# Second mixer: merge gates projected between the products of the linear attention's levels, gates kept in a slot of the weight ring

## The chip, the cores and the metric

The kernel runs on one core of a Trainium2 chip, in fp32 throughout. The metric is the device time of one execution in microseconds, the median of some runs. Five engines work side by side and wait for each other through semaphores: TensorE (PE: matmuls and transposes into PSUM), VectorE (DVE), ScalarE (ACT: functions and copies), GpSimd (POOL) and SyncE (SP), which issues nearly all transfers of weights from HBM. PSUM has 8 banks of 512 fp32 columns.

## The reference, cut to what matters

Two stacks of blocks run one after the other on 256 tokens of width 1024. The second has one layer: a hybrid mixer, then a mixture of 32 experts. The change touches the mixer alone:

```python
proj = jnp.concatenate([hc, hx], axis=1) @ w_in          # q k v | zd | b a | hq | f (2 directions) | hi | hz | gates (2 x 1024)
odn  = deltanet scans of q, k, v, b, a                    # gated delta rule, both directions
ohg  = gla scans of hq, f, hi (tokens in column order)    # HGRN2, both directions
br_dn = gated_rmsnorm(odn, zd, dn_norm_g) @ w_br_dn
br_hg = gated_rmsnorm(ohg, hz, hg_norm_g) @ w_br_hg
y = (sigmoid(gate_dn) * br_dn + sigmoid(gate_hg) * br_hg) @ w_out
x = x + mod_x[2] * y                                      # then norm, router, 32 experts (2 per token)
```

`silu(z)` gates each normed output, the two `sigmoid` gates (1024 columns each) weigh the two branches before the output projection. The gates depend on the layer's input alone, not on the scans.

## The kernel before, in words

**Weights.** `ring` has six slots of 2 MB. Every weight block of the mixer is one load of 2048 KB by SyncE into slot number mod 6, in the order of `plan2`: k, v, q, zd, hq, f0, hi, f1, hz, gd0, gd1, gh0, gh1, brd, brh, wo0, wo1 (`COL` gives the columns of w_in). A load waits for the reader of what was in its slot before (`READ`, the pair behind each entry); SyncE takes the loads strictly in order. Slots 0 to 2 are also the working memory (`spare`) of half the deltanet chunks, so loads into them wait for `S_ready` 6. After the plan come the experts' blocks (`main_pairs`): six blocks for each pair of experts, with eight places (`block_of`): the six slots in the order `SEQ`, and two areas of the arena. The first eight go as the places come free, each later one when the block eight before it has been read.

**Order of TensorE.** It is written out by hand. After the deltanet's ticks (the last work in them is `state` of chunk 3): zd (4 chains of 8 matmuls of 256 columns, banks 0 and 1), the sum of squares `o_ss`, hq (banks 4, 5), then for each direction d: f (512 columns, banks 4 to 7); for d = 0 hi (banks 0 to 3), for d = 1 hz (banks 4, 5) and gd0 (6, 7); transposes of the decayed keys (`kdT_ready`, L1294) that ScalarE copies out as `kdTok`; the state sum (`Sg_sum`, bank 2); eight levels; `attX` (L1323, bank 3); the output sum `og` (banks 0, 1). A level l is 8 products of 128x128 (L1316) into banks 4, 5 or 6, 7. For it GpSimd makes differences of log decays (L2573), ScalarE their exponentials, VectorE multiplies queries and keys with them (L2011, L2012: `W_ready`) and takes the product over into `attT` under the level's mask (L1994: `att_masked`). After the second direction: `o_ss` (L1339), the gates gd1, gh0, gh1 (banks 2, 3 or 0, 1), which ScalarE passes through the sigmoid one by one into `sgt`, an area of the arena, then the branch products brd and brh (each 8 chains of 4 matmuls), the broadcast of a row (L1364), and wo0, wo1. The norm, the router and the pairs of experts (L832 up, L847 down) follow.

**Semaphores.** `SHARED` lists, engine by engine, the order of increments of shared semaphores. `at(name, n)` is the value at the n-th increment of name.

All chains of matmuls are recorded with L645, the helper `chain`, all activations with L2100 or L2108, the helper `act`. The profile records each fp32 matmul of the code as two instructions: a chain set of 4 x 8 matmuls is x64.

## Time and profile before

| | us |
|---|---|
| time, median of 3 runs | 2647.0 (2645.55 to 2647.83) |
| span of the profiled execution | 2639.2 |
| TensorE busy | 2448.5 (93%) |
| VectorE busy | 616.0 (23%) |
| ScalarE busy | 380.9 (14%) |
| GpSimd busy | 157.4 (6%) |
| second mixer from zd on, brd at | 1757.7 to 2032.8 |

The span is taken from the first to the last instruction in one execution under the profiler; that execution's own device time isn't given, and the runs' median stands 7.8 us above its span. Busy shares are averages over stages with different limits, so a stage is read from its own stretch of the timeline. In a timeline a bracket holds the idle time of the engine before the row and the engine that ended it.

### The profile page before, as it was taken

The page shows a single profiled execution, that of the slowest core. Times are in us where ns is not written, and L with a number is a line of the kernel's source. Part 1 is how long each engine was busy: PE and PEld are TensorE (multiplying, and loading weights), DVE is VectorE, ACT ScalarE, POOL GpSimd, SP SyncE. Part 2 cuts the span into 40 slices and gives each one's busy share as a digit, 9 for nine tenths or more (in the row PEclk, how much of TensorE's full clock was granted, in tenths as well). Part 3 has the DMA queues.
Part 4 walks back from the last instruction along what each step waited for, and adds up shares of the span by engine and source line. Part 5 has one row for each costly group of instructions (what it writes and reads, how often), then busy time and mean ns, then how long its engine had stood idle before and what let it go on. Part 6 is the DMA issues. An engine that isn't in the chain of part 4 may idle for free.

```text
span 2639.2 us, 52419 instructions
## 1 busy us (share of the span) xinstructions
PE 2448.5 (93%) x24386; PEld 1581.1 (60%) x24386; DVE 616.0 (23%) x1160; ACT 380.9 (14%) x620; POOL 157.4 (6%) x145
## 2 busy tenths in 40 slices
PE   7889997899999999999998989999879889999997
PEld 5647776566666565656665678894568544444443
DVE  1730002101001010100000357632451332222223
ACT  1320102000000000000001342222141100000001
POOL 2000000000000000000000025420220100000000
PEclk9989998899999999999999989999999989999999
DMA  8773524599999999999999000031021479999995
GB/s 304 258 284 129 191 68 171 217 393 351 383 357 350 393 349 393 350 393 349 394 350 367 19 1 1 1 128 64 33 96 64 174 280 399 400 401 400 400 399 198
DMA packets 273271, 676.44 MB, mean 256 GB/s; under 512 B 5891, under 2 KB 9438, under 8 KB 268830
## 3 DMA queue, kind: packets, MB, share of 16 engines
q1 hardware_dynamic: 270624, 666.91, 67.2%
q0 software_dynamic: 2112, 6.04, 0.7%
q8 instruction: 196, 3.21, 0.5%
q14 instruction: 21, 0.17, 0.0%
q10 hardware_dynamic: 318, 0.10, 0.0%
HBM read 671.98 MB, written 1.05 MB: 255 GB/s over the span
## 4 chain that ended last, share of the span: by engine, by line
PE 78%; SPq 8%; DVE 6%; DMA 3%; ACT 3%; issue 1%; POOL 1%; DVEq 0%; ACTq 0%; POOLq 0%
PE ps L645 27%; PE ps L739 22%; PE ps L760 11%; SPq L596 8%; PE ps L832 4%; PE ps L1027 3%; PE ps L847 2%; ACT arena L2100 2%; DMA arena<-in_w_exp_up 2%; PE ps L820 1%; PE ps L1160 1%; PE ps L1172 1%; PE ps L746 1%; PE ps L1170 1%; PE ps L722 1%
## 5 line engine op out<-in xcount | busy, mean ns | idle before, releaser
L739 PE MATMUL ps<-ring,arena 128*32 128x256 f32 x10752 | 591.6, 379 | 1.1 <-DVE arena L1772 1.1
L739 PEld LDWEIGHTS ps<-ring,arena 128*32 128x32 f32 x10752 | 344.4, 110 | 231.7 <-issue 8.1
L645 PE MATMUL ps<-hT,ring 128*128 128x256 f32 (+1 forms) x1792 | 442.7, 408 | 20.1 <-ACT arena L2100 7.3
L2100 ACT ACTIVATE arena<-ps 128x384 f32<-128x384 f32 (+5 forms) x311 | 164.9, 550 | 1789.1 <-PE ps L739 558.8
L645 PEld LDWEIGHTS ps<-hT,ring 128*128 128x128 f32 x1792 | 345.1, 193 | 120.9 <-issue 69.7
L760 PE MATMUL ps<-ring,arena 128*32 128x256 f32 x5376 | 300.5, 379 | 0.0
L760 PEld LDWEIGHTS ps<-ring,arena 128*32 128x32 f32 x5376 | 173.9, 110 | 115.3 <-issue 1.3
L1504 DVE TENSOR_TENSOR arena<-arena,ps 128x384 f32<-128x384 f32 x56 | 31.0, 554 | 802.7 <-ACT arena L2100 802.7
L832 PE MATMUL ps<-ring,arena 128*64 128x512 f32 x768 | 168.8, 593 | 17.3 <-DMA ring<-in_w_exp_up 14.5
L645 PE MATMUL ps<-arena 128*128 128x128 f32 (+1 forms) x1064 | 133.5, 287 | 15.9 <-ACT arena L2100 5.1
L645 PEld LDWEIGHTS ps<-arena 128*128 128x128 f32 x1064 | 129.9, 203 | 17.6 <-ACT arena L2100 5.6
L832 PEld LDWEIGHTS ps<-ring,arena 128*64 128x64 f32 x768 | 57.8, 137 | 125.6 <-issue 122.6
L2513 POOL TENSOR_TENSOR ring<-ring,table 128x512 f32<-128x512 f32 x24 | 34.0, 1439 | 1139.3 <-ACT ring L2100 1104.8
L847 PE MATMUL ps<-ring,arena 128*64 128x512 f32 x384 | 85.0, 595 | 0.0
L1555 DVE TENSOR_TENSOR table<-arena,ps 128x512 f32<-128x512 f32 x16 | 11.0, 687 | 292.0 <-PE ps L832 292.0
L1027 PE MATMUL ps<-ring,arena 128*128 128x512 f32 x176 | 79.0, 592 | 0.0
L2100 ACT ACTIVATE arena<-arena 128x512 f32<-128x512 f32 (+4 forms) x71 | 58.4, 861 | 119.9 <-POOL arena L2573 30.4
L832 PE MATMUL ps<-arena 128*64 128x512 f32 x256 | 61.5, 637 | 7.8 <-DMA arena<-in_w_exp_up 7.8
L645 PE MATMUL ps<-ring,arena 128*128 128x512 f32 (+2 forms) x176 | 61.5, 506 | 6.6 <-ACT hT L2100 6.6
L820 PE MATMUL ps<-arena 128*128 128x512 f32 x136 | 62.9, 605 | 1.1 <-ACT arena L2100 1.1
L1721 DVE TENSOR_TENSOR arena<-arena,ps 128x256 f32<-128x256 f32 x22 | 9.3, 421 | 207.6 <-ACT arena L2100 207.6
L2084 DVE TENSOR_SCALAR arena<-ps,small 128x128 f32<-128x128 f32 x136 | 44.9, 402 | 54.7 <-PE ps L811 54.7
(364 smaller groups left out, 1920.2 us busy)
## 6 DMA issues: line engine op xcount, KB each, us to landing
ring<-in_moe_wg SPq DMA_DIRECT2D x56, 2048.0 KB, 11.3
ring<-in_moe_wu SPq DMA_DIRECT2D x56, 2048.0 KB, 16.3
ring<-in_moe_wd SPq DMA_DIRECT2D x56, 2048.0 KB, 17.1
ring<-in_w_exp_gate SPq DMA_DIRECT2D x24, 2048.0 KB, 23.3
ring<-in_w_exp_up SPq DMA_DIRECT2D x24, 2048.0 KB, 19.8
ring<-in_w_exp_down SPq DMA_DIRECT2D x24, 2048.0 KB, 19.1
ring<-in_w_in SPq DMA_DIRECT2D x13, 2048.0 KB, 10.1
ring<-in_w_ada SPq DMA_DIRECT2D x12, 2048.0 KB, 13.6
```

What stands on the lines that cost most here:

```text
L596: sp.dma_start(dst, w[2 * p + j, :, :].rearrange(rows_, p=P)).then_inc(inc("loaded%d" % b), 16)
L645: last = mm(outp, l, r, start=(i == 0), stop=(i == n - 1))
L739: last = mm(flat[32 * q:32 * q + 32, S * r:S * r + S], x_[:, k, 32 * r:32 * r + 32], gu[:, :, k, q * P:(q + 1) * P], start=(k == 0), stop= ...
L760: last = mm(flat[32 * q:32 * q + 32, 3 * 512 + S * r:3 * 512 + S * r + S], un_actT[:, c, r, :], d_[:, c, q * S:(q + 1) * S], start=(j == 0 ...
L820: last = mm(ps[:, (6 if t == 0 else 4) + c, :], GcT[:, 1 - b, t, :], ysb[:, c * 512:(c + 1) * 512], start=True, stop=True)
L832: last = mm(ps[64 * j:64 * j + 64, part, :], x_[:, k, 64 * j:64 * j + 64], w_[j][:, k, :], start=(k == 0), stop=(k == KC - 1))
L847: last = mm(ps[64 * j:64 * j + 64, 4 + h_, :], pr_actT[:, c, 64 * j:64 * j + 64], w_[j][:, c, h_ * 512:(h_ + 1) * 512], start=(c == 0), st ...
L1027: last = mm(ps[:, 4 + 2 * t + c, :], actb[:, (n - 1) % 4, t * P:(t + 1) * P], d_[:, j, c * 512:(c + 1) * 512], start=(n == 1), stop=(n == ...
L1504: V.tensor_tensor(un_act, un_sg, up_, ALU.mult).then_inc(inc("m1_act"), 1)
L2084: last = V.tensor_scalar(x_[:, c, :], ps[:, 2 + b, k * C:(k + 1) * C], gM[:, c:c + 1], mod[:, 24 + c, 0:1], ALU.mult, ALU.add)
L2100: return nc.scalar.activation(*a, **k)
L2513: G.tensor_tensor(WK[s_][d][2 + l % 2], WK[s_][d][1], rep(level_mask(l, d == 0), 4), ALU.mult)\
```

## The change

1. zd waits for `S_ready` 6 in place of 8.
2. f's four chains go in the order 2, 3, 0, 1, and for d = 0 the wait for `hq_ready` stands before chain 0 only.
3. In each direction the gate block (gd0, then gh0) is projected between the levels: after the products of each level come 4 of its 32 matmuls, into banks 0, 1. ScalarE copies the result, without the sigmoid, behind its levels' exponentials (`gate_kept`), and `og` waits for that copy.
4. In d = 1, hz moves to banks 0, 1 and gd1 to banks 2, 3, both directly behind f1 (their wait is now for `og_ready` 1); the transposes then wait for `z_silu` 2, and ScalarE copies gd1 out before kdTok.
5. gh1 is the one gate left behind the levels, half of it in front of `o_ss`. One sigmoid goes over the three kept gates in place, one more over gh1.
6. The gates live in slot 5 of the ring, which carries no weights in the mixer: `plan2` gets an entry without a source at each sixth place, so every block from f0 on has another slot. `SEQ` of the experts' first blocks and the counts for them change with that. The product with the row uses `ytmp` in the arena.

The tables in `SHARED` follow the new order and are not shown.

```diff
@@ -384,9 +384,10 @@
         zh = hT[:, 0:4, S:2 * S]
-        gd0 = hT[:, 4:8, S:2 * S]
         yhg = area(0, 4, S)
-        sgt = area(8192, 16, S)
+        GATES = 5
+        sgt = ring[:, GATES, :].rearrange("p (m s) -> p m s", m=16)
+        ytmp = area(8192, 8, S)
         mg = area(12288, KC, S)
@@ -432,16 +433,19 @@
         number = {e[0]: i for i, e in enumerate(plan)}
-        COL = {"k": 512, "v": 1024, "q": 0, "zd": 1536, "hq": 2064, "f0": 2576, "hi": 3600, "f1": 3088, "hz": 4112,
-               "gd0": 4624, "gd1": 5136, "gh0": 5648, "gh1": 6160}
+        COL = {"k": 512, "v": 1024, "q": 0, "zd": 1536, "hq": 2064, "f0": 2576, "hi": 3600, "gd0": 4624, "f1": 3088,
+               "hz": 4112, "gd1": 5136, "gh0": 5648, "gh1": 6160}
         READ = {"k": ("S_ready", 6), "v": ("S_ready", 6), "q": ("S_ready", 6), "zd": ("zd_proj", 1), "hq": ("hq_proj", 1),
...
                 "gd0": ("gate_proj", 1), "gd1": ("gate_proj", 2), "gh0": ("gate_proj", 3), "gh1": ("gate_proj", 4)}
-        plan2 = [(n, *cols("w_in_2", c), READ[n]) for n, c in COL.items()]
-        plan2 += [("brd", *rows("w_br_dn_2", 0, 4), ("br", 4)), ("brh", *rows("w_br_hg_2", 0, 4), ("br", 8))]
-        plan2 += [("wo%d" % i, *cols("w_out_2", 512 * i), ("y2_ready", i + 1)) for i in range(2)]
-        while len(plan2) % NSLOT:
-            plan2.append(("padb%d" % len(plan2), None, 0, 0, ("y2_ready", 1)))
+        weights2 = [(n, *cols("w_in_2", c), READ[n]) for n, c in COL.items()]
+        weights2 += [("brd", *rows("w_br_dn_2", 0, 4), ("br", 4)), ("brh", *rows("w_br_hg_2", 0, 4), ("br", 8))]
+        weights2 += [("wo%d" % i, *cols("w_out_2", 512 * i), ("y2_ready", i + 1)) for i in range(2)]
+        plan2 = []
+        for entry_ in weights2:
+            if len(plan2) % NSLOT == GATES:
+                plan2.append(("gates%d" % len(plan2), None, 0, 0, ("mg_ready", 1) if entry_[0] == "wo0" else ("q_proj", 1)))
+            plan2.append(entry_)
         P2 = M1 + 3 * UNITS
@@ -475,7 +479,11 @@
-        SEQ = (0, 3, 1, 4, 2, 5, 6, 7)
+        SEQ = (2, 3, 4, 5, 0, 1, 6, 7)
+
+        def loads_before(b):
+
+            return sum(1 for i in range(M2) if i % NSLOT == b)
@@ -794,7 +802,7 @@
                     block_, b, use = block_of(6 * p + 2 * part + j)
-                    pe.wait_ge(*at("loaded%d" % b, ((M2 // NSLOT if b < NSLOT else 0) + use) * 16 + 16))
+                    pe.wait_ge(*at("loaded%d" % b, (loads_before(b) + use) * 16 + 16))
                     return block_.rearrange("p (k n) -> p k n", k=k)
@@ -1241,7 +1249,7 @@
             w = take("zd")
-            pe.wait_ge(*at("S_ready", 8))
+            pe.wait_ge(*at("S_ready", 6))
             for m in range(4):
@@ -1256,13 +1264,17 @@
             last.then_inc(inc("hq_proj"), 1)
+            def gate(w, b, m):
+                return chain(ps[:, b + m // 2, (m % 2) * S:(m % 2 + 1) * S],
+                             [(w[:, k, m * P:(m + 1) * P], hTx[:, k, :]) for k in range(KC)])
+
             for d in range(2):
                 w = take("f%d" % d)
-                if d == 0:
-                    pe.wait_ge(*at("hq_ready", 1))
-                else:
+                if d == 1:
                     pe.wait_ge(*at("att_masked", 8))
-                for m in range(4):
+                for m in (2, 3, 0, 1):
+                    if d == 0 and m == 0:
+                        pe.wait_ge(*at("hq_ready", 1))
                     last = chain(ps[:, 4 + m, :], [(w[:, k, m * P:(m + 1) * P], hT[:, k, :]) for k in range(KC)])
@@ -1278,14 +1290,16 @@
                 else:
-                    pe.wait_ge(*at("f_sig", 2))
-                    for b, name in ((4, "hz"), (6, "gd0")):
-                        w = take(name)
-                        for m in range(4):
-                            last = chain(ps[:, b + m // 2, (m % 2) * S:(m % 2 + 1) * S],
-                                         [(w[:, k, m * P:(m + 1) * P], hTx[:, k, :]) for k in range(KC)])
-                        last.then_inc(inc("hz_proj" if b == 4 else "gate_proj"), 1)
                     pe.wait_ge(*at("og_ready", 1))
+                    w = take("hz")
+                    for m in range(4):
+                        last = gate(w, 0, m)
+                    last.then_inc(inc("hz_proj"), 1)
+                    w = take("gd1")
+                    for m in range(4):
+                        last = gate(w, 2, m)
+                    last.then_inc(inc("gate_proj"), 1)
+                    pe.wait_ge(*at("z_silu", 2))
@@ -1294,15 +1308,16 @@
                 pe.wait_ge(*at("kdTok_ready", d + 1))
+                if d == 1:
+                    pe.wait_ge(*at("gate_kept", 2))
                 for h in range(H):
...
+                w = take(("gd0", "gh0")[d])
                 for l in range(8):
...
                     n = 8 * d + l
-                    if d == 1 and l < 2:
-                        pe.wait_ge(*(at("z_silu", 2) if l == 0 else at("gate_sig", 1)))
                     if l == 0:
@@ -1316,6 +1331,11 @@
                     last.then_inc(inc("att_ready"), 1)
+                    m = l // 2
+                    for k in range(4 * (l % 2), 4 * (l % 2) + 4):
+                        last = mm(ps[:, m // 2, (m % 2) * S:(m % 2 + 1) * S], w[:, k, m * P:(m + 1) * P], hTx[:, k, :],
+                                  start=(k == 0), stop=(k == KC - 1))
+                last.then_inc(inc("gate_proj"), 1)
                 pe.wait_ge(*at("W_ready", 8 * d + 8))
@@ -1326,6 +1346,7 @@
                 pe.wait_ge(*at("qe_ready", d + 1))
+                pe.wait_ge(*at("gate_kept", 2 * d + 1))
                 for t in range(NT):
@@ -1333,20 +1354,16 @@
                 last.then_inc(inc("og_sum"), 1)
-            pe.wait_ge(*at("og_ready", 2))
+            w = take("gh1")
+            pe.wait_ge(*at("attX_ready", 2))
+            gate(w, 2, 0)
+            gate(w, 2, 1)
             pe.wait_ge(*at("o_sq", 2))
...
             last.then_inc(inc("o_ss"), 1)
-
-            for i, name in ((1, "gd1"), (2, "gh0"), (3, "gh1")):
-                w = take(name)
-                if i >= 3:
-                    pe.wait_ge(*at("gate_sig", i - 1))
-                for m in range(4):
-                    last = chain(ps[:, 2 * (i % 2) + m // 2, (m % 2) * S:(m % 2 + 1) * S],
-                                 [(w[:, k, m * P:(m + 1) * P], hTx[:, k, :]) for k in range(KC)])
-                last.then_inc(inc("gate_proj"), 1)
+            gate(w, 2, 2)
+            gate(w, 2, 3).then_inc(inc("gate_proj"), 1)
             pe.wait_ge(*at("rs_done", 2))
@@ -1359,7 +1376,6 @@
             pe.wait_ge(*at("dg_ready", 1))
-            pe.wait_ge(*at("gate_sig", 4))
             for i in range(2):
@@ -2033,11 +2049,10 @@
             done(last, "dg_ready")
-            ve.wait_ge(*at("gate_sig", 4))
+            ve.wait_ge(*at("gate_sig", 2))
             for c in range(4):
                 ve.wait_ge(*at("br", c + 1))
-                gate = gd0[:, 2 * c:2 * c + 2, :] if c < 2 else sgt[:, 2 * c:2 * c + 2, :]
-                done(V.tensor_tensor(mg[:, 2 * c:2 * c + 2, :], bank(4 + c, 2, S), gate, ALU.mult), "br_read")
+                done(V.tensor_tensor(mg[:, 2 * c:2 * c + 2, :], bank(4 + c, 2, S), sgt[:, 2 * c:2 * c + 2, :], ALU.mult), "br_read")
             for c in range(4):
@@ -2049,10 +2064,10 @@
                 for t in range(NT):
-                    done(V.tensor_tensor(sgt[:, 2 * (2 * n + t):2 * (2 * n + t) + 2, :], bank(4 + 2 * n + t, 2, S),
+                    done(V.tensor_tensor(ytmp[:, 2 * (2 * n + t):2 * (2 * n + t) + 2, :], bank(4 + 2 * n + t, 2, S),
                                          grow[:, n * 512:(n + 1) * 512].rearrange("p (a b) -> p a b", a=2), ALU.mult))
                     last = V.tensor_tensor(res[:, t, n * 512:(n + 1) * 512], res[:, t, n * 512:(n + 1) * 512],
-                                           sgt[:, 2 * (2 * n + t):2 * (2 * n + t) + 2, :].rearrange("p a b -> p (a b)"), ALU.add)
+                                           ytmp[:, 2 * (2 * n + t):2 * (2 * n + t) + 2, :].rearrange("p a b -> p (a b)"), ALU.add)
                     if n and t == 0:
@@ -2432,11 +2447,11 @@
                     for h in range(H):
-                        last = act(zh[:, h, :].rearrange("p (c r) -> p c r", r=4), permuted(ps[:, 4 + h // 2, (h % 2) * S:(h % 2 + 1) * S]), ACT.Silu)
+                        last = act(zh[:, h, :].rearrange("p (c r) -> p c r", r=4), permuted(ps[:, h // 2, (h % 2) * S:(h % 2 + 1) * S]), ACT.Silu)
                     done(last, "z_silu")
-                    ac.wait_ge(*at("gate_proj", 1))
-                    done(act(gd0, ps[:, 6:8, :].rearrange("p b (h q) -> p (b h) q", h=2), ACT.Sigmoid), "gate_sig")
                     functions(EXP)
+                    ac.wait_ge(*at("gate_proj", 2))
+                    act(sgt[:, 4:8, :], ps[:, 2:4, :].rearrange("p b (h q) -> p (b h) q", h=2), ACT.Copy).then_inc(inc("gate_kept"), 1)
                 ac.wait_ge(*at("kdT_ready", d + 1))
@@ -2444,6 +2459,8 @@
                     act(w_[:, :, d, :], w_[:, :, d, :], ACT.Exp, scale=-1.0).then_inc(inc("W_exp"), 1)
+                ac.wait_ge(*at("gate_proj", 2 * d + 1))
+                act(sgt[:, 8 * d:8 * d + 4, :], ps[:, 0:2, :].rearrange("p b (h q) -> p (b h) q", h=2), ACT.Copy).then_inc(inc("gate_kept"), 1)
             functions(LN)
@@ -2452,11 +2469,10 @@
             functions(SIG)
-            ac.wait_ge(*at("y_gated", 2))
-            for i in range(1, 4):
-                ac.wait_ge(*at("gate_proj", i + 1))
-                done(act(sgt[:, 4 * i:4 * i + 4, :], ps[:, 2 * (i % 2):2 * (i % 2) + 2, :].rearrange("p b (h q) -> p (b h) q", h=2),
-                         ACT.Sigmoid), "gate_sig")
+            ac.wait_ge(*at("gate_kept", 3))
+            done(act(sgt[:, 0:12, :], sgt[:, 0:12, :], ACT.Sigmoid), "gate_sig")
+            ac.wait_ge(*at("gate_proj", 4))
+            done(act(sgt[:, 12:16, :], ps[:, 2:4, :].rearrange("p b (h q) -> p (b h) q", h=2), ACT.Sigmoid), "gate_sig")
             ac.wait_ge(*at("grow_sum", 1))
```

## Rows read from the trace of the kernel before

**Rows 1.** The page of the kernel before: span, and chain that ended last by engine.
```profile
span 2639.2 us, 52419 instructions
...
PE 78%; SPq 8%; DVE 6%; DMA 3%; ACT 3%; issue 1%; POOL 1%; DVEq 0%; ACTq 0%; POOLq 0%
```

**Rows 2.** Timeline of TensorE: start, us, instructions, count, idle before and its releaser.
```profile
1757.69 14.05 PE L645 MATMUL ps<-hT,ring 128*128 128x256 f32 x64 [2.25 <-DVE arena L1909]
...
1789.99 29.40 PE L645 MATMUL ps<-hT,ring 128*128 128x512 f32 x64 [2.72 <-ACT arena L2100]
1819.23 13.90 PE L645 MATMUL ps<-ring,arena 128*128 128x512 f32 x32
...
1849.60 1.06 PE L1294 MATMUL ps<-table,arena 128*128 128x128 f32 x8 [2.73 <-DVE arena L1978]
1851.83 3.56 PE L645 MATMUL ps<-arena 128*128 128x128 f32 x16 [1.17 <-ACT arena L2100]
1855.18 2.12 PE L1316 MATMUL ps<-arena 128*128 128x128 f32 x16
...
1879.15 1.16 PE L1323 MATMUL ps<-arena 128*128 128x128 f32 x8 [0.53 <-DVE arena L2012]
1881.16 4.73 PE L645 MATMUL ps<-arena 128*128 128x128 f32 x40 [0.85 <-DVE arena L2015]
1885.73 27.63 PE L645 MATMUL ps<-hT,ring 128*128 128x512 f32 x64
1917.98 30.74 PE L645 MATMUL ps<-hT,ring 128*128 128x256 f32 x128 [4.62 <-ACT arena L2100]
1948.57 1.04 PE L1294 MATMUL ps<-table,arena 128*128 128x128 f32 x8
1953.52 2.90 PE L645 MATMUL ps<-arena 128*128 128x128 f32 x16 [3.92 <-ACT arena L2100]
1956.22 4.56 PE L1316 MATMUL ps<-arena 128*128 128x128 f32 x32
...
1980.18 1.16 PE L1323 MATMUL ps<-arena 128*128 128x128 f32 x8 [0.52 <-DVE arena L2012]
...
1989.54 1.95 PE L1339 MATMUL ps<-arena,table 128*128 128x512 f32 x4 [2.62 <-ACT arena L2100]
1991.34 41.60 PE L645 MATMUL ps<-hT,ring 128*128 128x256 f32 x192
2032.78 17.43 PE L645 MATMUL ps<-arena,ring 128*128 128x256 f32 x80
```

**Rows 3.** Windows: stretch, length, busy us of each engine, granted clock, DMA share, GB/s.
```profile
1921.00:1924.00 3.00, 3.00 (x9) 2.35 (x9) 2.93 (x4) 0.00 (x0) 0.00 (x0) 0.53 0.00 0
...
1964.00:1969.00 5.00, 2.88 (x23) 2.69 (x24) 4.97 (x8) 2.10 (x4) 2.77 (x2) 1.00 0.00 0
```

**Rows 4.** Windows, TensorE alone, between the second mixer and the experts' end.
```profile
2120.00:2137.00 17.00, 13.04 (x68) 0.85 0.09 34
...
2170.00:2600.00 430.00, 407.65 (x1986) 0.99 1.04 400
```

**Rows 5.** Timeline of ScalarE, the second direction and the second norm.
```profile
1936.29 2.79 ACT L2100 ACTIVATE arena<-arena 128x256 f32<-128x256 f32 x5 [5.92 <-DVE arena L1971]
1939.10 1.28 ACT L2100 ACT_TABLE_LOAD   x1
1940.40 1.21 ACT L2100 ACTIVATE hT<-ps 128x256 f32<-128x256 f32 x4
...
1952.44 1.02 ACT L2100 ACTIVATE arena<-ps 128x1024 f32<-128x1024 f32 x1
...
1994.02 1.06 ACT L2100 ACTIVATE arena<-arena 128x1024 f32<-128x1024 f32 x1
```

**Rows 6.** SyncE's loads released by S_ready 6: start, us, instructions.
```profile
1726.40 4.39 SPq L500 DMA_DIRECT2D ring<-in_w_in  x3
```

**Rows 7.** DMA issues of 1725 to 1732: KB each, median us to landing.
```profile
ring<-in_w_in SPq DMA_DIRECT2D x3, 2048.0 KB, 14.0
```

10 lines of the change are left out of this document (5 added, 5 removed).

## The prediction

> **What bounds the kernel now.** I read four views. The page comes first: the span is 2639.2 us, and the chain that ended last is TensorE for 78%, with SyncE's transfers a distant second [rows 1]. So time is won only by taking TensorE work off the chain or by filling TensorE's waits. Second, TensorE's own order of time through the second mixer [rows 2]. The reader is to see the idle time in brackets, where an engine waited, and the durations of equal pieces of work, which tell the clock. The waits of some size are: 2.25 us before zd, 2.72 before f0, 2.73 and 1.17 around the first key transposes, 4.62 before hz and gd0, 3.92 before the second Sg sum, 2.62 before the second o_ss. In the bracket of levels TensorE works 2.05 us and then waits about 1.1 us, eight times in each direction. At the end the gates gd1, gh0, gh1 run alone for 41.6 us.
>
> Third, the windows [rows 3]. In the levels VectorE is busy 4.97 of 5.00 us and TensorE 2.88 of 5: there VectorE sets the pace and TensorE has room. After the wait of 4.62 us the granted clock is 0.53, nearly all at the lower level, 1.2 GHz; in the levels it is 1.00, 2.4 GHz, although TensorE waits in each of them. Fourth, what follows the mixer [rows 4]. From 2120 to 2137 the transfers stand nearly still (DMA share 0.09): all eight blocks of weights are there and wait for the first pair of experts. From then on the DMA engines are full, 400 GB/s. That stream starts when the first pair's gate product frees its blocks, so if TensorE arrives there some us earlier, stream and end move by as much. I therefore count the change at the start of the brd product, at 2032.78, and carry the difference over one to one.
>
> **The change, part by part.** The units first [rows 2]. 192 recorded matmuls of 128x256 take 41.60 us, 0.217 each, so that one gate projection (64 recorded) is 13.87; 40 recorded matmuls of 128x128 take 1885.73 - 1881.16 = 4.57 us up to the next start, 0.114 each, so that the products of a level (16 recorded) are 1.83.
>
> (a) zd waits for S_ready 6 instead of 8. Its banks 0 and 1 belong to the third chunk, done long before. The work in front ends as before, so the 2.25 us go. What was waiting behind it (o_ss, which still needs ScalarE's square) comes 13.9 us later and finds that done. Gain 2.25.
>
> (b) f0 begins with m = 2, 3 (banks 6, 7) and waits for hq_ready only before m = 0, after 13.8 us of work. ScalarE's part took only the 2.72 us of the wait, so it is hidden. With the wait goes the low clock: f0 took 29.40, the same work for f1 27.63. Gain 2.72 + 1.77 = 4.5. If the cover were gone, it would cost these 4.5 again. VectorE, ScalarE and GpSimdE behind f0 (sigmoids, logs, scans, kd) all start from f0 or hi and shift with it, so the waits of 2.73 and 1.17 us and the slow Sg sum (3.56 us) stay.
>
> (c) Half a chain of gd0 (4 matmuls, 8 recorded: 1.73 us) goes behind each level's products. TensorE now needs 1.83 + 1.73 = 3.56 us a level, more than VectorE's pace (first product to attX: 1879.15 - 1855.18 = 23.97, 3.0 a level), so TensorE becomes the bound: 8 x 3.56 = 28.5. Cost 4.5. Does the loop through VectorE break this? A level's product ends, VectorE masks (1.3) and multiplies (2.0), and the product after next needs that; two levels are 7.1 us, the loop 2.05 + 1.3 + 2.0 = 5.4. It has 1.7 us of room. The pace can't be below the 3.56 of TensorE's own work; its upper bound is 4.0, if each change of form paid the pipeline's tail that 2.05 shows over 1.83, twice. The gate is copied by ScalarE (1.02 us as the kdTok copy, of the same size) while attX is made: og follows attX's start by 2.01 us, so it is covered by 0.8; uncovered it would be a wait of 1.
>
> (d) Between f1 and hz the wait for f_sig goes, because hz now writes banks 0 and 1, which VectorE reads out right after the first direction's og. Before: f1 ends at 1913.36, hz and gd0 end at 1948.57, 35.2 us. After: hz and gd1 without a wait or low clock, 27.7. Gain 7.5. The place of gd0 is taken by gd1, at the same price.
>
> (e) The wait then is for ScalarE. Its chain runs from f_sig: eg_exp ends at 1939.08, 25.7 us after f1's end; then come a table load 1.28 and z_silu 1.21, to 28.25 [rows 5]. TensorE is ready at 27.7, waits 0.6, transposes (1.04). ScalarE loads the exponential's table (1.28, to 29.5), copies gd1 out (1.02, to 30.6) and only then kdTok (to 31.6), which the Sg sum waits for. This is the new wait behind an added instruction: about 2.2 us. Sg sum 1.83, so the first level starts at 33.5 after f1's end, 5.8 after gd1's. Before it was 1956.22 - 1948.57 = 7.65. But these two waits, with only the transposes between them, may lower the clock: waits of 2.72, 3.92 and 4.62 us did (slow work stands behind each), the one of 2.62 did not (the gates behind it take 0.217 each as everywhere). The price is between 0 and 1.8 (Sg sum at 3.56 against 1.83); I take 1.8, since the two together are nearest the 2.73 and 1.17 of the first direction, which had it. Gain 0. The Trainium skill (ScalarE: Activation LUTs, section What ACT_TABLE_LOAD costs) puts a switch of table at 1283 ns and a drain of 1380 ns more. The trace shows 1.28 us and the next activation 0.02 us behind; by the page the Sg sum would come 1.4 us later and the gain would be an estimated 34.
>
> (f) The second direction's levels take gh0: cost 4.5 again. The wait for z_silu and gate_sig before the first two falls away.
>
> (g) From attX of the second direction to brd: before 2032.78 - 1980.18 = 52.6. After: 2.01 to og, og 4.57, half of gh1 6.93, o_ss 1.8, other half 6.93: 22.2. The half in front of o_ss covers the 2.62 us in which VectorE adds og and ScalarE squares it. Gain 30.4 (gd1 and gh0 are gone from here: 27.7; the wait 2.6). Is brd held up otherwise? rs_done came 5.54 after o_ss's start (1995.08 - 1989.54 [rows 2, 5]): 19.1 after attX, three before brd. Then table load 1.28, one sigmoid over 3072 columns (at most 3 x 1.06), the last 1.06: 24.6; VectorE needs it when the first brd chain ends, at 25.7. And even 5 us late it would hold up only brh, which comes 14 us later.
>
> (h) Transfers. Slot 5 holds the gates, f0 moves to slot 0, so it is loaded only at S_ready 6 (1726.4 [rows 6], landing after about 14 us for three of them [rows 7]) and needed at 1785: 44 us to spare. Every later block has its slot free at least 50 us before its use. All loads are on SyncE's queue, and none waits there behind one that is later than before. The experts' first blocks go to slots 2, 3, 4, 5, which are free with gate_proj 4, br 4, br 8 and mg_ready, three of them earlier than now; but they were all in by 2120 anyway, so this is worth 0. ytmp in place of sgt, and VectorE's reads from the ring: 0, same sizes.
>
> Sum: 2.25 + 4.5 - 4.5 + 7.5 + 0 - 4.5 + 30.4 = 35.65 us. The execution that was profiled has a span of 2639.2, and would have 2603.6; the median of the runs, 2647.0, lies 7.8 above the span, so that I forecast 2647.0 - 35.6 = 2611.4.
>
> **Rivals.** (A) The forecast: gates inside the levels at 3.5 to 4.0 us a level. Chance 0.85. Its own range: a gain of 35.6 + 1.8 + 1.8 = 39.2 if the clock holds in (e) and, with other times of arrival, behind the first direction's waits too; one of 35.6 - 7 - 1.3 = 27.3 if the pace is 4.0 (2 x 8 x 0.44) and the drop in (e) costs as much as that behind the 4.62 us (30.74 - 27.63 = 3.1 in place of 1.8). That is 2608 to 2620, and with the 2 us by which the runs differ 2606 to 2622.
>
> (B) The half chains are not hidden: TensorE starts them when it could have started the next product and VectorE idles as long, 3.0 + 1.73 a level. Against it stand 1.1 us of idle in each level and the room in the loop. Levels then cost 13.8 each instead of 4.5: gain 17, 2630. Chance 0.07.
>
> (C) The end does not follow the mixer, because the experts' stream, bound by DMA from 2137 on, can't start earlier. The 17 us before 2137, with idle DMA engines [rows 4], speak against it; it would give 2647. Chance 0.03.
>
> (D) Slower: the clock. Both brackets of levels begin right after TensorE's longest remaining waits. If the engine stayed at 1.2 GHz there, two brackets of 28.5 us would take as much again: 57 - 35.6 = 21 us slower, 2668. It decides from 36 us of full-speed work done at the low level. The rows show at most 3.1 us lost behind a wait, some 6 us at the low level, and 1.00 in the levels [rows 2, 3]. The Trainium skill (TensorE: Matmul & The Clock Gate, section Seeing it yourself) reports that the gate was seen stuck low for over 50 us; no row here shows it. Chance 0.03. Unknown causes of a loss, such as a wait that I placed wrong: 0.02.
>
> **The numbers.** A measurement of this kernel tells about 0.2% (5 us) from no change. Faster: A and B and nearly nothing else, 0.92; same: C, 0.03; slower: 0.05. The range is 2606 to 2622, A's own.
>
> **What would show it.** In the trace after: zd directly behind the last state product; f0 without a wait and in 27.7 us; 3.5 to 3.6 us between the products of two levels, VectorE waiting for TensorE there; no idle between f1 and hz; about 0.6 and 2.2 us of idle around the second transposes; 22 us from the second attX to brd, 52.6 before; the first pair of experts earlier by the full sum. It is wrong if VectorE still sets the levels' pace at over 4 us, if the clock falls in new places, or if the distance from brd to the end grows.

## The result and the profile after

The changed kernel takes 2609.3 us (median of 4 runs, 2601.6 to 2610.7) against 2646.3 for the one before (4 runs, 2640.9 to 2647.8). The ratio is 0.9855, with an interval of 0.9836 to 0.9875: 37 us by the medians, 1.5%. The profiled execution of the changed kernel has a span of 2599.7 us, the one before 2639.2 [rows 1]: 39.5 us less.

The timeline of TensorE through the second mixer, kernel after (start, us, instruction, count, idle before; L653 is now `chain`, L1331 a level's products, L1336 the gate's matmuls in the levels, L1343 attX, L1308 the transposes):

```profile
1753.69 13.98 PE L653 MATMUL ps<-hT,ring 128*128 128x256 f32 x64
...
1769.22 41.44 PE L653 MATMUL ps<-hT,ring 128*128 128x256 f32 x128
...
1840.87 1.94 PE L1308 MATMUL ps<-table,arena 128*128 128x128 f32 x8 [2.74 <-DVE arena L1994]
1843.98 3.53 PE L653 MATMUL ps<-arena 128*128 128x128 f32 x16 [1.17 <-ACT arena L2115]
1847.35 1.95 PE L1331 MATMUL ps<-arena 128*128 128x128 f32 x16
1849.13 1.89 PE L1336 MATMUL ps<-hT,ring 128*128 128x256 f32 x8
1850.86 1.95 PE L1331 MATMUL ps<-arena 128*128 128x128 f32 x16
...
1875.46 1.05 PE L1343 MATMUL ps<-arena 128*128 128x128 f32 x8
1877.36 4.73 PE L653 MATMUL ps<-arena 128*128 128x128 f32 x40 [0.85 <-DVE arena L2031]
1881.93 55.26 PE L653 MATMUL ps<-hT,ring 128*128 128x512 f32 x192
1937.87 1.09 PE L1308 MATMUL ps<-table,arena 128*128 128x128 f32 x8 [0.68 <-ACT hT L2115]
1941.12 2.05 PE L653 MATMUL ps<-arena 128*128 128x128 f32 x16 [2.16 <-ACT arena L2115]
1943.01 1.95 PE L1331 MATMUL ps<-arena 128*128 128x128 f32 x16
...
1971.12 1.05 PE L1343 MATMUL ps<-arena 128*128 128x128 f32 x8
...
1977.59 7.07 PE L653 MATMUL ps<-hT,ring 128*128 128x256 f32 x32
1984.50 1.88 PE L1363 MATMUL ps<-arena,table 128*128 128x512 f32 x4
...
1993.12 27.14 PE L653 MATMUL ps<-arena,ring 128*128 128x256 f32 x125
```

Read beside [rows 2]: the brackets of 2.25, 2.72, 4.62 and 2.62 us are gone, and with them the stretched durations behind two of them: hq and f0 are one piece of 41.44 us without a wait. From the first product of a level to the next is 3.51 us (1850.86 - 1847.35), 1.78 for the products and 1.73 for the gate, and there is no bracket between them in any of the sixteen levels. f1, hz and gd1 are one piece of 55.26 us. From the second attX to brd it is 22.0 us, where it was 52.6. What is left are the waits of 2.74 and 1.17 us in the first direction, 0.68 and 2.16 in the second.

The windows of the kernel after (busy us of PE, PEld, DVE, ACT, POOL; granted clock; DMA share; GB/s):

```profile
1950.00:1970.00 20.00, 20.00 (x140) 18.89 (x140) 15.41 (x23) 5.76 (x10) 8.23 (x5) 1.00 0.00 1
...
2137.00:2560.00 423.00, 400.65 (x1963) 178.60 (x1964) 100.44 (x264) 36.44 (x56) 0.00 (x0) 0.99 1.04 400
```

In the levels TensorE is busy all of the 20 us and VectorE 15.4, where VectorE was full and TensorE had 2.88 of 5 [rows 3]: the two have changed places. The clock is 1.00, 2.4 GHz. The experts run as before, DMA engines full at 400 GB/s [rows 4].

ScalarE in the second direction, and in front of brd, kernel after:

```profile
1935.31 1.28 ACT L2115 ACT_TABLE_LOAD   x1
1936.60 1.21 ACT L2115 ACTIVATE hT<-ps 128x256 f32<-128x256 f32 x4
1937.83 1.28 ACT L2123 ACT_TABLE_LOAD   x1
1939.13 1.02 ACT L2115 ACTIVATE ring<-ps 128x1024 f32<-128x1024 f32 x1
1940.05 1.02 ACT L2115 ACTIVATE arena<-ps 128x1024 f32<-128x1024 f32 x1
...
1991.28 2.77 ACT L2115 ACTIVATE ring<-ring 128x3072 f32<-128x3072 f32 x1
1994.07 1.02 ACT L2115 ACTIVATE ring<-ps 128x1024 f32<-128x1024 f32 x1
```

The table load for z_silu, z_silu, the load of the exponential's table, the copy of gd1 and the copy of kdTok stand one behind the other, and the Sg sum starts at 1941.12, when the last is done. The one sigmoid over 3072 columns takes 2.77 us.

All traces can be cut at the same places. Starts of TensorE's work, from the last product of deltanet to brd, in us:

| stretch | before | after | difference |
|---|---|---|---|
| last deltanet product to zd | 3.31 | 0.89 | -2.42 |
| zd to hi | 61.54 | 56.81 | -4.73 |
| hi to the transposes | 30.37 | 30.37 | 0 |
| transposes to the first level | 5.58 | 6.48 | +0.90 |
| levels to attX | 23.97 | 28.11 | +4.14 |
| attX to f1 | 6.58 | 6.47 | -0.11 |
| f1 to the transposes | 62.84 | 55.94 | -6.90 |
| transposes to the first level | 7.65 | 5.14 | -2.51 |
| levels to attX | 23.96 | 28.11 | +4.15 |
| attX to brd | 52.60 | 22.00 | -30.60 |
| sum | 278.40 | 240.32 | -38.08 |
| brd to the end | 606.4 | 606.6 | +0.2 |

So the gain is in the mixer, and the 606 us behind it moved as a block. The rest of the 39.5 lies ahead of zd, where TensorE's work was not changed: the last deltanet product starts at 1754.38 before and at 1752.80 after.

### The profile page after: what moved, and what is told of

Its sections match the earlier page's. It is cut to its first block, busy times and chain, and to the rows that moved or that the text cites. A ratio compares the mean times of both kernels' runs of the same rounds, so it can differ in the third digit from the quotient of the medians.

```text
span 2599.7 us, 52418 instructions
## 1 busy us (share of the span) xinstructions
PE 2437.1 (94%) x24386; PEld 1575.2 (61%) x24386; DVE 613.5 (24%) x1160; ACT 382.4 (15%) x620; POOL 157.5 (6%) x145
## 3 DMA queue, kind: packets, MB, share of 16 engines
q8 instruction: 196, 3.21, 0.5%
## 4 chain that ended last, share of the span: by engine, by line
PE 80%; SPq 8%; DVE 6%; DMA 3%; ACT 2%; issue 1%; DVEq 0%; ACTq 0%; POOLq 0%
PE ps L653 25%; PE ps L747 23%; PE ps L768 11%; SPq L604 8%; PE ps L840 4%; PE ps L1035 3%; DMA ring<-in_w_exp_up 2%; PE ps L855 2%; ACT arena L2115 1%; PE ps L828 1%; PE ps L1168 1%; PE ps L1331 1%; PE ps L1336 1%; PE ps L1180 1%; PE ps L754 1%
## 5 line engine op out<-in xcount | busy, mean ns | idle before, releaser
L653 PE MATMUL ps<-hT,ring 128*128 128x256 f32 (+1 forms) x1664 | 408.7, 405 | 10.5 <-issue 6.8
L653 PEld LDWEIGHTS ps<-hT,ring 128*128 128x128 f32 x1664 | 317.2, 191 | 104.8 <-issue 63.5
L653 PE MATMUL ps<-arena 128*128 128x128 f32 (+1 forms) x1064 | 132.7, 286 | 14.1 <-DVE arena L1548 3.7
L653 PEld LDWEIGHTS ps<-arena 128*128 128x128 f32 x1064 | 129.3, 202 | 16.0 <-ACT arena L2115 4.0
L653 PE MATMUL ps<-ring,arena 128*128 128x512 f32 (+2 forms) x176 | 61.5, 506 | 6.6 <-ACT hT L2115 6.6
## 6 DMA issues: line engine op xcount, KB each, us to landing
ring<-in_w_exp_down SPq DMA_DIRECT2D x24, 2048.0 KB, 19.2
```

The source lines that it names most:

```text
L653: last = mm(outp, l, r, start=(i == 0), stop=(i == n - 1))
```

## The experiments

Each was run on the chip with a profile and timed beside the kernel before, whose median lay between 2646.2 and 2646.8 us. As the times of one kernel differ by some 8 us from run to run and several parts are smaller, the stretch from the last deltanet product to brd is given for each; the time is beside it.

| kernel | stretch to brd | against after | time, us | ratio to before |
|---|---|---|---|---|
| before | 278.4 | +38.1 | 2646.8 | 1 |
| after | 240.3 | 0 | 2609.3 | 0.9855 (0.9836 to 0.9875) |
| after, once more | 240.3 | 0 | 2609.0 | 0.9866 (0.9848 to 0.9885) |
| gates ahead of the levels | 259.5 | +19.2 | 2625.0 | 0.9917 (0.9900 to 0.9934) |
| levels without gates | 232.1 | -8.2 | 2596.1 | 0.9806 (0.9787 to 0.9825) |
| hz waits for f_sig | 245.6 | +5.3 | 2610.5 | 0.9868 (0.9844 to 0.9891) |
| o_ss ahead of gh1 | 244.8 | +4.5 | 2610.0 | 0.9867 (0.9850 to 0.9883) |
| experts' blocks late | 240.3 | 0 | 2607.1 | 0.9860 (0.9841 to 0.9879) |
| before, zd alone | 275.6 | | 2643.3 | 0.9986 (0.9976 to 0.9996) |
| before, f0 alone | 275.3 | | 2644.8 | 0.9994 (0.9984 to 1.0004) |
| transposes in banks 4, 5 | 238.6 | -1.7 | 2605.8 | 0.9849 (0.9835 to 0.9864) |
| the same, table load late | 234.4 | -5.9 | 2601.2 | 0.9826 (0.9813 to 0.9838) |
| the same, once more | 234.4 | -5.9 | 2603.2 | 0.9835 (0.9818 to 0.9852) |
| the same, half chain in the wait | 233.1 | -7.3 | 2603.1 | 0.9833 (0.9818 to 0.9848) |

### Is the gain of the gates their place between the products?

The changed kernel, with each gate in one piece ahead of its levels:

```diff
                 w = take(("gd0", "gh0")[d])
+                for m in range(4):
+                    last = gate(w, 0, m)
+                last.then_inc(inc("gate_proj"), 1)
                 for l in range(8):
...
-                    m = l // 2
-                    for k in range(4 * (l % 2), 4 * (l % 2) + 4):
-                        last = mm(ps[:, m // 2, (m % 2) * S:(m % 2 + 1) * S], w[:, k, m * P:(m + 1) * P], hTx[:, k, :],
-                                  start=(k == 0), stop=(k == KC - 1))
-                last.then_inc(inc("gate_proj"), 1)
```

> The changed kernel with the gates gd0 and gh0 projected in one piece (64 recorded matmuls, 13.87 us) between the Sg sum and the first level, not between the levels. Theory (the waits inside the levels hide most of the gate): from the first product to attX the stretch returns from 28.1 to about 24.0 us, but 13.87 us stand in front of it, so each direction is 13.87 - 4.15 = 9.7 us longer, 19.4 in both: about 2628 against 2609 for the changed kernel and 2646 for the one before. Rival (the placement inside the levels is worth little, the gain comes from the removed waits): within 5 us of the changed kernel, 2609 to 2614.

The timeline of TensorE in this kernel (L1334 are the products of the levels):

```profile
1855.47 13.98 PE L653 MATMUL ps<-hT,ring 128*128 128x256 f32 x64
1869.29 3.73 PE L1334 MATMUL ps<-arena 128*128 128x128 f32 x32
1873.95 2.05 PE L1334 MATMUL ps<-arena 128*128 128x128 f32 x16 [0.92 <-DVE arena L2026]
...
1892.40 1.16 PE L1341 MATMUL ps<-arena 128*128 128x128 f32 x8 [0.53 <-DVE arena L2026]
```

The gate takes 13.82 us (1869.29 - 1855.47), and then the waits of 0.9 to 1.2 us in each level are back. From the start of the gate to attX it is 36.9 us, against 28.1: 8.8 more in each direction. With a slower Sg sum in the second (below) it makes 19.2 us, and 16 by the median times. Expected were 19.4, as 9.7 in each direction: the levels behind the gate take 23.1 us and not 24.0 (the first two follow each other without a wait), and the slower Sg sum adds 1.4, so that the near agreement of the sum is partly luck. The rival, with under 5, is out: the place between the products hides about two thirds of each gate.

The second, without the gates in the levels (gd0 and gh0 are left out but for one matmul in each direction):

```diff
-                    m = l // 2
-                    for k in range(4 * (l % 2), 4 * (l % 2) + 4):
-                        last = mm(ps[:, m // 2, (m % 2) * S:(m % 2 + 1) * S], w[:, k, m * P:(m + 1) * P], hTx[:, k, :],
-                                  start=(k == 0), stop=(k == KC - 1))
+                last = mm(ps[:, 0, 0:S], w[:, 0, 0:P], hTx[:, 0, :], start=True, stop=True)
                 last.then_inc(inc("gate_proj"), 1)
```

> The changed kernel without the gate matmuls in the levels (gd0 and gh0 are left out but for one matmul in each direction, so two of the four gates are not computed). Theory (VectorE sets the pace of bare levels at 3.0 us, TensorE with the gates at 3.51): the stretch from the first product to attX goes from 28.1 back to about 24.0 + 0.2, 8.0 us in both directions: about 2601. Rival (the levels' pace in the changed kernel is set by something else than TensorE's own work, such as a wait on VectorE behind the gates): the stretch stays over 26 us, the time within 4 us of 2609.

A window inside its levels:

```profile
1858.00:1878.00 20.00, 13.32 (x107) 12.18 (x106) 19.76 (x26) 6.89 (x12) 10.89 (x6) 1.00 0.00 0
```

VectorE is busy 19.76 of 20 us again and TensorE 13.32. The levels' stretch is 23.9 us, as in the kernel before, and the sum 8.2 us less than in the changed kernel. So the two gates in the levels cost 8.3 us of the 27.7 that they take alone, and the pace of 3.51 is TensorE's own work and nothing else. The time falls by more than that, 13 us by the medians; in the profile nothing over 8.2 is in the mixer, and the runs' spread (2591.9 to 2603.2 here) covers the rest.

### Do the removed waits give what they took?

hz waits for the sigmoids of f again:

```diff
                     pe.wait_ge(*at("og_ready", 1))
                     w = take("hz")
+                    pe.wait_ge(*at("f_sig", 2))
```

> The changed kernel with one wait put back: hz waits for f_sig 2 again, as before the change, although its banks don't need it. Theory (term d): TensorE idles 4.6 us behind f1 and loses some 3.1 us more at the lower clock, so hz and gd1 end 7.7 us later; ScalarE's chain to z_silu ends 28.25 us behind f1 whatever TensorE does but for gd1, so the wait before the transposes (0.7) is swallowed and so is part of the one before the Sg sum, whose copies need gd1 at 27.7 + 7.7 = 35.4: net 35.4 + 1.1 (copy) + 1.0 (kdTok) = 37.5 against 31.6 behind f1 for the start of the Sg sum: 5.9 us, 2615. Rival (the clock is not part of it): idle 4.6 but hz and gd1 in 27.7 us, net 2.8 us, 2612.

```profile
1921.57 30.09 PE L653 MATMUL ps<-hT,ring 128*128 128x256 f32 x128 [4.71 <-ACT arena L2116]
...
1953.68 2.05 PE L653 MATMUL ps<-arena 128*128 128x128 f32 x16 [1.15 <-ACT arena L2116]
```

The wait is 4.71 us and hz and gd1 then take 30.09 where 27.6 is their time at the full clock: 2.4 us at the lower level, so the clock is part of it. From f1 to the Sg sum it is 64.5 us against 59.2. Of the 7.1 us that TensorE lost, ScalarE's chain swallows 1.8, as its two waits shrink from 0.68 and 2.16 to none and 1.15. The forecast was 5.9, the rival without the clock had 2.8; 5.3 it is. The timing cannot show it: 0.9868 with an interval of 0.0047 is as well that of the changed kernel.

o_ss in front of all of gh1:

```diff
-            gate(w, 2, 0)
-            gate(w, 2, 1)
             pe.wait_ge(*at("o_sq", 2))
...
+            gate(w, 2, 0)
+            gate(w, 2, 1)
             gate(w, 2, 2)
             gate(w, 2, 3).then_inc(inc("gate_proj"), 1)
```

> The changed kernel with o_ss in front of all of gh1, as before the change, instead of behind its first half. Theory (term g): TensorE waits 2.6 us for VectorE's og and ScalarE's square, and the distance from the second attX to brd grows from 22.0 to 24.6 us: 2612. No clock penalty, as none stood behind this wait before. Rival: with the busier levels in front the clock falls here too and costs up to 1.8 us more, 2613.5; or brd is held up by rs_done anyway, then no growth.

```profile
1980.49 3.58 PE L1361 MATMUL ps<-arena,table 128*128 128x512 f32 x4 [2.63 <-ACT arena L2115]
1983.90 13.98 PE L653 MATMUL ps<-hT,ring 128*128 128x256 f32 x64
```

The wait of 2.63 us is back and o_ss takes 3.58 us, where it took 1.95 behind the same wait in the kernel before [rows 2]. The windows of this kernel say why, the clock of TensorE is 0.57 there:

```profile
1980.00:1984.00 4.00, 3.51 (x5) 0.57 0.00 0
1984.00:1990.00 6.00, 6.00 (x30) 1.00 0.00 0
```

So the rival is right in this profile: 2.6 of waiting and 1.7 at the lower level (3.41 us from the start of o_ss to the next work, 1.72 in the changed kernel), together nearly all of the 4.5 us. Its reason, the busier levels in front, is not shown: the kernel with f0 alone, below, has the levels of before and the same fall. Again the timing alone would not have told it.

The first two parts were done alone on the kernel before, each in a kernel of its own:

```diff
-            pe.wait_ge(*at("S_ready", 8))
+            pe.wait_ge(*at("S_ready", 6))
...
-                if d == 0:
-                    pe.wait_ge(*at("hq_ready", 1))
-                else:
+                if d == 1:
                     pe.wait_ge(*at("att_masked", 8))
-                for m in range(4):
+                for m in (2, 3, 0, 1):
+                    if d == 0 and m == 0:
+                        pe.wait_ge(*at("hq_ready", 1))
```

> The kernel before with one part of the change alone: zd waits for S_ready 6 instead of 8. Theory (term a): zd follows the last state product without a wait, 2.25 us and some 0.1 to 0.2 of slower work gained, and all behind it moves by as much: 2646.3 - 2.4 = 2644. Rival: ScalarE or the hq path swallows it, because hq_ready or hxp sets the start of f0 and hi: no change at brd.

> The kernel before with one part alone: f's chains in the order 2, 3, 0, 1 and the wait for hq_ready only before chain 0 of the first direction. Theory (term b): the 2.72 us of wait and the 1.77 us at the lower clock behind it go, hi starts 4.5 us earlier: 2642. Rival (the low clock has nothing to do with the wait): hi starts 2.7 us earlier, f0 still takes 29.4, 2643.6.

With zd alone the last deltanet product and zd stand 0.89 us apart as after the change: 2.42 us gained there, 2.8 to brd, 3.5 by the median times; the interval ends just under 1. With f0 alone, zd to hi goes from 61.54 to 56.88: 4.66 us, both terms, and the rival with 2.7 is out. But only 3.1 us arrive at brd, and 2 by the median times, where no change is within the interval. The trace shows where the rest went: behind the wait of 2.63 in front of the second o_ss the clock fell in this run (attX to brd 54.3 us against 52.6). The other stretches differ too, by TensorE's clock, and nearly cancel: the first transposes to the first level take 0.8 us more, the second ones 0.6 more, and hz and gd0 behind the same wait of 4.62 us take 29.28 us against 30.74.

### Do the experts' early blocks matter?

```diff
                             elif free[b]:
-                                sp.wait_ge(*at(*free[b]))
+                                sp.wait_ge(*at(*(("y2_ready", 1) if n in (1, 2, 3) else free[b])))
```

> The changed kernel with the experts' blocks 1, 2 and 3 loaded only when wo0 has been read, as late as before the change, though their slots are free 14 to 30 us earlier. Theory (term h): all eight blocks still land before the first pair begins, so the distance from brd to the end stays at 606 and the time at 2609. Rival: the early loads are part of the gain, because the later ones (or the router's small loads) queue behind them: brd to the end grows by 2 to 5 us.

> The changed kernel once more, beside its variants on the same chip. Theory: mixer as in its first profile, 22.0 us from the second attX to brd and 28.1 in each direction's levels; about 2609. The clock behind the waits of 0.7 and 2.2 us around the second transposes may be full as in the first profile or low (1.4 us more), since other kernels with the same waits show both.

The loads on SyncE's queue, first in the changed kernel (its second run), then in this one (start, us, instruction):

```profile
1993.45 14.18 SPq L604 DMA_DIRECT2D ring<-in_w_exp_gate  x2
2021.08 1.89 SPq L604 DMA_DIRECT2D ring<-in_w_exp_up  x2
```

```profile
1995.06 43.58 SPq L604 DMA_DIRECT2D ring<-in_w_exp_gate  x2
2038.68 5.10 SPq L604 DMA_DIRECT2D ring<-in_w_exp_up  x2
```

In the changed kernel the second gate block is asked for 14 us behind the first and the up blocks around 2021; here the second one waits until 2038.6. From brd to the end it is 606.7 us here and 608.1 in the changed kernel beside it, and the median times are 2607.1 and 2609.0. In all fourteen profiles this distance lies between 605.5 and 608.8 us; this run's is in the midst of them, and the 2 to 5 us of the rival are not to be seen. The early blocks are worth nothing that these runs could show.

### What is left, and a faster version

The two remaining pairs of waits are around the transposes. They need banks 0 and 1, which hi's copies hold in the first direction and z_silu in the second. Banks 4 and 5 have been free since the sigmoids of f:

```diff
                 pe.wait_ge(*at("kd_ready", d + 1))
-                pe.wait_ge(*at("hv_ready", 1))
                 for t in range(NT):
                     for h in range(H):
-                        last = nc.tensor.transpose(ps[:, t, h * P:(h + 1) * P], Wd[:, h, t * P:(t + 1) * P], ident)
+                        last = nc.tensor.transpose(ps[:, 4 + t, h * P:(h + 1) * P], Wd[:, h, t * P:(t + 1) * P], ident)
                 last.then_inc(inc("kdT_ready"), 1)
+                pe.wait_ge(*at("hv_ready", 1))
                 pe.wait_ge(*at("kdTok_ready", d + 1))
                 if d == 1:
+                    pe.wait_ge(*at("z_silu", 2))
                     pe.wait_ge(*at("gate_kept", 2))
...
-                done(act(kdTok, ps[:, 0:2, :].rearrange("p t (h q) -> p t h q", h=H), ACT.Copy), "kdTok_ready")
+                done(act(kdTok, ps[:, 4:6, :].rearrange("p t (h q) -> p t h q", h=H), ACT.Copy), "kdTok_ready")
```

> The changed kernel with the transposes of the decayed keys in banks 4 and 5 instead of 0 and 1 (f's sigmoids have read these, and the first level's products come after kdTok), so that they wait neither for hv_ready nor for z_silu 2; the Sg sum waits for both. Theory: the waits around the transposes are due to the banks. First direction: from hi's end to the first product 2.7 + 6.5 = 9.2 us in the changed kernel; now the Sg sum is free when hv is copied, 2.6 us behind hi, and the first product 1.8 us later: 4.5 us, if the clock holds; 4.7 us gained, 2.9 if the clock still falls. Second direction: transposes directly behind gd1 but ScalarE's copies in the same order, gain 0 to 0.2. Sum 3 to 5 us: 2604.5 to 2606.5. Rival (VectorE's work in that stretch is what TensorE waits for, kd and hv both): gain below 1 us.

The first direction gives what was expected: hi to the first level is 32.2 us against 36.9, a gain of 4.7. The second loses 3.0 where 0 to 0.2 were to be gained, so that the sum is 1.7 and not 3 to 5. The reason is in two lines:

```profile
1943.60 3.75 PE L653 MATMUL ps<-arena 128*128 128x128 f32 x16 [3.10 <-ACT arena L2115]
...
1947.15 3.21 PE L1331 MATMUL ps<-arena 128*128 128x128 f32 x16
```

The transposes come at once, but the Sg sum still waits for ScalarE's copies; the two waits of 0.7 and 2.2 us have become one of 3.10, and behind it the Sg sum takes 3.75 (2.05 at the full clock) and the first level's products 3.21 (1.95). So TensorE arrived earlier and had more to wait. The next version takes the table load out of the way of the copies:

```diff
                     done(last, "z_silu")
-                    functions(EXP)
...
                 done(act(kdTok, ps[:, 4:6, :].rearrange("p t (h q) -> p t h q", h=H), ACT.Copy), "kdTok_ready")
+                if d == 1:
+                    functions(EXP)
```

> As i1_banks45, and ScalarE loads the exponential's table in the second direction after it has copied gd1 and kdTok, not before. Theory: the copies need no table of their own, so the Sg sum of the second direction comes 1.2 us earlier than in i1_banks45 and the first exponentials come no later: 2603 to 2605. Rival: the load has to stand before the copies or another load appears, or the first level then waits for VectorE's product with the later exponential: no difference from i1_banks45.

> The version with the key transposes in banks 4 and 5 and the late table load, once more and beside the changed kernel on the same chip. Theory: 6 us less than the changed kernel in the mixer (4.7 in the first direction, 1.3 in the second), 2603 against 2609. Rival (the difference of its first timing was the chip's): within 2 us of the changed kernel.

TensorE in the first direction and ScalarE in the second, in the second run of this kernel:

```profile
1839.77 1.09 PE L1306 MATMUL ps<-table,arena 128*128 128x128 f32 x8
1842.53 2.05 PE L653 MATMUL ps<-arena 128*128 128x128 f32 x16 [1.66 <-DVE arena L1994]
1844.42 1.95 PE L1331 MATMUL ps<-arena 128*128 128x128 f32 x16
```

```profile
1933.68 1.21 ACT L2115 ACTIVATE hT<-ps 128x256 f32<-128x256 f32 x4
1934.92 1.02 ACT L2115 ACTIVATE ring<-ps 128x1024 f32<-128x1024 f32 x1
1935.84 1.02 ACT L2115 ACTIVATE arena<-ps 128x1024 f32<-128x1024 f32 x1
1936.88 1.28 ACT L2123 ACT_TABLE_LOAD   x1
```

In the first direction one wait of 1.66 us is left and all work runs at the full clock. In the second, both copies stand directly behind z_silu and the load after them; a wait of 1.82 us stays in front of the Sg sum. Over the version with the early load, 1.2 us were expected from this and 4.2 came: 1.3 by the load, and 2.9 because the Sg sum (2.02 us) and the first products (1.95) run at the full clock again. The mixer is 5.9 us shorter than in the changed kernel, in both runs of it, and on the same chip the medians are 2603.2 and 2609.0. The intervals of the ratios, 0.9818 to 0.9852 and 0.9848 to 0.9885, just overlap, so the 6 us rest on the traces and both medians, not on the timing alone.

The last puts a half chain of gh0 into the second direction's wait. `part(i)` is the i-th of the eight half chains of a gate, 4 matmuls:

```diff
                 last.then_inc(inc("kdT_ready"), 1)
+                w = take(("gd0", "gh0")[d])
+                if d == 1:
+                    pe.wait_ge(*at("z_silu", 2))
+                    part(0)
...
+                    if l + d < 8:
+                        last = part(l + d)
```

> The same version, and in the second direction the first half chain of gh0 (1.73 us) goes between the transposes and the Sg sum, where TensorE waits about 1.8 us for ScalarE's copies, and not behind the first level; the eighth level carries no gate work. Theory: the wait takes it, the levels with gates are one fewer, and the levels' stretch goes from 28.1 to about 26.4: 1.7 us gained, and the clock has less reason to fall. 2601. Rival: z_silu comes so late that the half chain starts only when the Sg sum could, then it delays this by what the levels give back: no difference.

```profile
1941.08 1.97 PE L1313 MATMUL ps<-hT,ring 128*128 128x256 f32 x8
1943.01 2.02 PE L653 MATMUL ps<-arena 128*128 128x128 f32 x16
```

The half chain stands in the wait, the Sg sum comes no later (2.86 us behind the start of the transposes, 2.85 without it), and the levels' stretch is 26.4 us. So 1.7 us are gained, as expected. Of them 0.4 is lost again before og, which waits 1.25 us for VectorE's attX instead of 0.85. The mixer is 1.3 us shorter than without it; the time does not show it.

## Why the prediction was right

The forecast was 2611.4 and the measured median 2609.3; in the mixer 35.65 us were forecast, and 38.1 came; the medians differ by 37.0. The terms came one by one, so the agreement is not luck, except that the two that were off, 1.8 us gained in (e) and 0.9 lost in front of the first direction's levels, partly cancel.

- (a) and (b) were 2.25 and 4.5, and measured 2.42 and 4.73 in the changed kernel, 2.42 and 4.66 when done alone. That part of (b) was the clock and not the wait is shown by the second.
- (c) and (f): 4.5 of cost each, measured 4.14 and 4.15. TensorE became the bound as was said; the pace is 3.51 and not 3.56, because the products of a level take 1.78 and not the 1.83 that I took from og's different mix. Rival (B), gates that aren't hidden, is out with the two experiments on their place. The prediction reads the waits in the levels too broadly: about 1.1 us of idle time stands before six of the eight levels of each direction and not before all, which its sum does not use.
- (d): 7.5, measured 7.6 (from f1 to the end of gd1 55.3 us against 62.8).
- (e) is the term that was off: 0 was forecast and 1.8 came. The times of arrival were right (waits of 0.68 and 2.16 against 0.6 and 2.2), but I had charged 1.8 us for the clock, and it held. It was a choice between two bounds, and the runs show that both occur: with these same two waits in front the Sg sum ran at full clock in five profiles (after, twice, and three variants) and at the lower level in one (3.41 us in the version with the gates ahead). The trace shows a table load of 1.28 us and the next activation right behind it also here, so the drain that the Trainium skill puts on top (ScalarE: Activation LUTs, section What ACT_TABLE_LOAD costs) is not in this path: its 1.4 us, behind the load of the exponential's table alone, would have made the Sg sum start at about 1942.5, and it started at 1941.12.
- A cost that I had not seen: in the first direction the transposes themselves, which took 1.06 us [rows 2], take 1.94. The granted clock during them is 0.50 after the change and 1.00 before, behind the same wait of 2.7 us: the low clock begins one piece earlier, which costs 0.9 us. Why it does so is open; with zd alone they took 1.06, with f0 alone 1.63.
- (g): 30.4, measured 30.6; the sigmoids were in time (1994.07 + 1.02 = 1995.1, and the first brd chains end at about 1996.6).
- (h): 0, as the late blocks cost nothing. Rival (C) is out with the 606 us that moved as a block.
- Rival (D), the clock: 1.00 in both brackets of levels, where TensorE is busy all of the 28.11 us. It lost nothing there.
- The way from the span to the time was wrong in its reason, without effect on the difference. I took the 7.8 us between the median and the span as something outside the span. The profiled execution of the kernel before took 2640.9 us, 1.7 over its span; it was faster than the other three runs by 5 to 7. Beside it, the profiled execution of the kernel after took 2601.6, which is 39.3 less. The profiles show two groups: the last deltanet product starts between 1752.8 and 1754.7 in seven of the fourteen (before and after among them) and between 1759.9 and 1760.9 in the other seven. The groups differ in TensorE's clock in the first mixer.

The same window in the kernel after and in the one with hz behind the sigmoids:

```profile
80.00:200.00 120.00, 97.38 (x501) 0.93 0.78 282
```

```profile
80.00:200.00 120.00, 102.27 (x490) 0.87 0.77 280
```

102.3 us of TensorE time against 97.4 within this window, at a clock of 0.87 against 0.93, in code that is the same in both. The seven early profiles all have 97.4 us here, the seven late ones 100.6 (two) or 102.3 (five), so this window holds 3 to 5 of the 5 to 8 us between the groups. The runs without a profile have no trace; that their spread of some 8 us, in which differences of 2 to 5 us are lost, has the same origin is likely but not shown.

## What to carry to other kernels

When one engine sets the pace of a loop with dependent steps, independent work of another engine can be cut into pieces of the size of its wait and put behind each step: here 27.7 us of gate projections cost 8.3. The pieces turn the bound around once they are larger than the wait (1.73 against 1.1 us), so what is over belongs into other waits. A wait that comes from a buffer's bank and not from data goes away with another bank, but look at once what the engine then runs into: taking away one wait in front of the transposes made the next one longer and slower, until the table load behind it was moved too. And measure parts of 2 to 5 us by the stretch in the trace, as the times of whole runs do not resolve them.

## What the hardware showed that was not expected

- The same wait costs the clock or does not, from one profile to the next. The wait of 2.6 us before the second o_ss was followed by full clock in the kernel before and in the one with zd alone (attX to brd 52.6 us in both), and by the lower level in the one with f0 alone (54.3) and in the one with o_ss ahead of gh1 (o_ss 3.58 us against 1.95). Waits of 0.68 and 2.16 us were followed by it in one profile of six. Behind the 2.73 and 1.17 of the first direction it fell in all ten profiles that had them. The size differs too: behind the same wait of 4.62 us, hz and gd0 take 30.74 us in the kernel before, 30.43 with zd alone and 29.28 with f0 alone. What decides between them is left open.
- VectorE's multiplication of the queries is held up while GpSimd's subtraction runs. The groups of VectorE's instructions in the first direction's levels (line, names, shapes, count | busy us, mean ns | idle before), kernel before and kernel after:

```profile
L2011 DVE TENSOR_TENSOR arena<-arena 128x512 f32<-128x512 f32 x8 | 9.1, 1136 | 0.3
```

```profile
L2027 DVE TENSOR_TENSOR arena<-arena 128x512 f32<-128x512 f32 x8 | 6.8, 846 | 0.3
```

It is the same instruction: 1136 ns before, 846 after. Single instructions of the kernel before show what stands behind the means:

```profile
1860.56 1.34 DVE L1994 COPY_PREDICATED arena<-table,ps 128x512 f32<-128x512 int32 x2
1860.72 2.01 POOL L2573 TENSOR_TENSOR arena<-arena 128x1024 f32<-128x1024 f32 x1 [1.23 <-DVE arena L2012]
1861.93 1.34 DVE L2011 TENSOR_TENSOR arena<-arena 128x512 f32<-128x512 f32 x1
...
1877.81 0.69 DVE L2011 TENSOR_TENSOR arena<-arena 128x512 f32<-128x512 f32 x1
```

Where GpSimd is idle the multiplication takes 0.69 us. In six levels of this direction it begins during the subtraction; there it takes 1.24 to 1.34 us and ends 0.54 to 0.55 us behind the subtraction's end each time (here 1863.27 and 1862.73). So it is the end of GpSimd's instruction that sets its length, not a lower rate of work. The masks, which read PSUM and a table, take their usual 0.67 us each beside the same subtraction. In the kernel after, only three levels of each direction meet so (1.29, 1.17 and 0.85 us, again with 0.54 to 0.55 behind the subtraction's end), and in the others the multiplication begins after it and takes 0.69. In the second direction of the version with the transposes in banks 4 and 5 none meets (mean 692 ns): its first level comes late by TensorE's low clock, and all others are paced by TensorE from the start. The bare level's 3.1 to 3.2 us thus hold up to 0.6 us of this meeting, and a level bound by TensorE leaves VectorE more room than the difference of the paces says.
